# Weight tiles in two transfers of 64 partitions each, in a one-core decoder layer

## The reference, cut to what matters

```
hn = rms_norm(x);   proj = hn @ w_in             # 2048 x 7184
... gated DeltaNet and retention heads on proj ...
h  = x + mixed @ w_out                           # 2048 x 2048
hn = rms_norm(h);   q = hn @ w_pq                # 2048 x 2048, then top 16 of product keys
h  = h + sum_k gelu(expert_u[idx_k] . hn) * gate_k * expert_v[idx_k]     # 16384 experts, 128 picked a token
h  = h + sigmoid(rms_norm(h) @ w_ple_gate) * (p @ w_ple_proj)
out = rms_norm(h)
```

## Time and profile before

| | |
|---|---|
| median of three runs | 2109.89 us (2107.45 to 2109.89) |
| profiled execution, whole | 2103.78 us |
| its span | 2101.9 us |
| TensorE busy | 2039.3 us, 97% |
| VectorE busy | 1638.5 us, 78% |
| ScalarE busy | 1084.8 us, 52% |
| read from HBM | 476.31 MB |
| mean rate of the transfers | 236 GB/s |

### The profile page before, as it was taken

How to read it: one execution, slowest core, us unless ns; L and a number is a source line. 1 busy time by engine, 2 the same in 40 slices (tenths; PEclk the granted TensorE clock), 3 DMA queues, 4 the chain that set the end, 5 groups by cost and what they waited for, 6 DMA issues and landing times.

```text
span 2101.9 us, 38248 instructions
## 1 busy us (share of the span) xinstructions
PE 2039.3 (97%) x12266; PEld 1869.2 (89%) x12266; DVE 1638.5 (78%) x2509; ACT 1084.8 (52%) x1450; POOL 725.3 (35%) x423
## 2 busy tenths in 40 slices
PE   7999999979999999999999999999999999999997
PEld 7888778878789999999999999999999899899785
DVE  6885777985567888888888666898889788888755
ACT  6543566334435755545554544555555555455454
POOL 0030200000001878788888860232323233343000
PEclk9999999999999999999999999999999999999999
DMA  5655558215555777777777776899999889999454
GB/s 196 254 185 184 171 170 298 103 55 206 183 178 176 213 205 208 212 208 209 210 202 209 216 245 244 317 350 348 350 344 346 299 306 330 351 332 341 171 182 138
DMA packets 171795, 496.19 MB, mean 236 GB/s; under 512 B 48560, under 2 KB 48976, under 8 KB 169808
## 3 DMA queue, kind: packets, MB, share of 16 engines
q1 hardware_dynamic: 117056, 413.39, 56.8%
q0 software_dynamic: 51200, 67.25, 12.0%
q10 hardware_dynamic: 3472, 14.78, 1.9%
HBM read 476.31 MB, written 19.04 MB: 236 GB/s over the span
## 4 chain that ended last, share of the span: by engine, by line
PE 81%; DVE 8%; DMA 6%; DVEq 2%; ACT 1%; issue 1%; ACTq 0%; SPq 0%
PE ps L261 27%; PE ps L266 15%; PE ps L1922 14%; PE ps L1927 8%; PE ps L287 5%; PE ps L281 5%; PE ps L282 5%; DMA raw<-in_v_table 4%; DVE lo L241 2%; ACT hi L235 1%; PE ps L363 1%; DMA arena<-in_u_table,few_pick 1%; DVE arena L1133 1%; DMA raw<-in_w_in_cols 1%; DVE arena L1468 1%
## 5 line engine op out<-in xcount | busy, mean ns | idle before, releaser
L235 ACT ACTIVATE hi<-raw 128x1024 fp32r<-128x1024 f32 x724 | 768.5, 1062 | 865.3 <-PE ps L261 387.1
L241 DVE TENSOR_TENSOR lo<-raw,hi 128x1024 fp32r<-128x1024 f32 x724 | 892.3, 1236 | 346.6 <-ACT hi L235 308.8
L261 PE MATMUL ps<-act_pair,hi 128*128 128x448 f32 (+1 forms) x2816 | 654.4, 374 | 0.0
L1653 POOL DMA_INDIRECT gate_map<-gate_in_sb x256 | 473.3, 1849 | 401.3 <-DVEq L1418 325.7
L261 PEld LDWEIGHTS ps<-act_pair,hi 128*128 128x128 f32 x2816 | 504.5, 189 | 49.2
L266 PEld LDWEIGHTS ps<-act_pair,lo 128*128 128x128 f32 x2816 | 372.0, 191 | 18.9 <-DVE lo L241 3.9
L266 PE MATMUL ps<-act_pair,lo 128*128 128x224 f32 (+1 forms) x2816 | 375.3, 276 | 1.9 <-DVE lo L241 1.9
L1922 PE MATMUL ps<-stage,hi 128*128 128x448 f32 x1024 | 232.1, 367 | 3.0 <-ACT hi L235 1.5
L1922 PE MATMUL ps<-act_pair,hi 128*128 128x448 f32 x1024 | 229.7, 366 | 1.9 <-ACT hi L235 1.9
L1670 POOL DMA_INDIRECT arena<-in_u_table,few_pick x64 | 104.4, 1631 | 304.3 <-DVE keep L1468 270.0
L1922 PEld LDWEIGHTS ps<-stage,hi 128*128 128x128 f32 x1024 | 183.1, 189 | 17.6 <-DVE gate_in_sb L1520 2.4
(11 more groups left out here) (254 smaller groups left out, 1678.0 us busy)
## 6 DMA issues: line engine op xcount, KB each, us to landing
raw<-in_expert_u SPq DMA_DIRECT2D x256, 512.0 KB
raw<-in_v_table SPq DMA_DIRECT2D x256, 512.0 KB
raw<-in_w_in_cols SPq DMA_DIRECT2D x64, 512.0 KB
raw<-in_w_in_rows SPq DMA_DIRECT2D x48, 512.0 KB
raw<-in_w_out SPq DMA_DIRECT2D x32, 512.0 KB
raw<-in_w_pq SPq DMA_DIRECT2D x32, 512.0 KB
raw<-in_w_gate SPq DMA_DIRECT2D x32, 512.0 KB
gate_map<-stage SPq DMA_DIRECT2D x1, 14336.0 KB, 41.2
```

The source lines that it names most:

```text
L235: act.activation(hi[:, use, :], raw[:, slot, :], ACT.Copy).then_inc(hi_ready, 1)
L241: dve.tensor_tensor(lo[:, use, :], raw[:, slot, :], hi[:, use, :].bitcast(F32), ALU.subtract).then_inc(lo_ready, 1)
L261: mm = pe.matmul(first_tokens(out_ap), hi[:, use, d8 * P:(d8 + 1) * P], first_tokens(act_pair[:, d, :]), start=(d == 0), stop=False)
L1653: pool.indirect_dma_start(gate_map, bass.IndirectOffsetOnAxis(ap=place[0:n, unit, r:r + 1], axis=0), gates_out[0:n, unit, r:r + 1], None, ...
```

## The change

Each weight tile is fetched by two transfers in place of one: partitions 0 to 63 and then partitions 64 to 127, 256 KB each, both on SyncE's queue and both on the buffer's semaphore. Each raises it by 16, so ScalarE waits for 32 a turn. The tile's place, its bytes, the wait ahead of the transfers and all of the other engines' work stay as they were.

```diff
         def load_tile(sp, n, slot, src, first=False):
             if not first:
                 sp.wait_ge(lo_ready, n - RAW + 1)
-            sp.dma_start(raw[:, slot, :], src).then_inc(weights_landed[slot], 16)
+            for part in range(2):
+                rowsl = slice(part * P // 2, (part + 1) * P // 2)
+                sp.dma_start(raw[rowsl, slot, :], src[rowsl]).then_inc(weights_landed[slot], 16)
 
         def round_tile(act, n, slot, use, turn, first=False):
-            act.wait_ge(weights_landed[slot], 16 * turn + 16)
+            act.wait_ge(weights_landed[slot], 32 * turn + 32)
             if not first:
                 act.wait_ge(hi_used, n - SPLIT + 1)
                 act.wait_ge(lo_ready, n - SPLIT + 1)
```

## The result

The changed kernel took 2324.19 us (median of four runs, 2306.31 to 2334.13) against 2108.67 us of the kernel before: a ratio of 1.101, with a 95% interval of 1.098 to 1.104. It is slower by about 215 us. The forecast of slower held. Its size, 95 us, did not: less than half of the loss was foreseen. That 2324 us lies just inside the likeliest case's 2140 to 2330 is owed to the width of that range and not to the sum.

The account below looks back on a forecast made before the run. TensorE was taken to bound the kernel, with transfers close behind in the second expert stage. Only engine time counted: 54 + 41 = 95 us on 2103.8, plus 4 for the median, gave 2203 us; range 2103 to 2330.

Parts of the forecast that it names:

- the likeliest case: Engine time of the halves shows in part, mainly in the second expert stage: 2140 to 2330 us, chance 0.50.
- What bounds the kernel, and where it shows: Whole kernel: TensorE, busy 97%, sets the pace; in the second expert stage transfers are close behind, DMA 0.95 and 0.91.
- SyncE: SyncE's queue: issues double to 1448, 0.5 us more a tile, covered by 2.2 us of standing still; 0 on the path.
- The later half: Every tile: upper half issued 0.5 us later, hidden by the 1.9 us reserve; taken as 0, at worst 44 us.
- more completions: Every tile: one more small packet per engine, at most 0.16 us a tile; taken as 0.
- The engine time of the bytes: DMA engines, every tile: bytes to few partitions hold an engine longer, 0.07 us per 4096 B, 0.55 us a tile.
- What of it lies on the path: Second expert stage: 0.55 us less idle 0.13 and 0.23 us, times 128 tiles each: 54 and 41 us, sum 95.
- The cover elsewhere: Outside the second expert stage: idle engine time hides the 0.55 us, barely in the first expert stage (0.63 us a tile).
- nothing happening: Whole kernel: rival that the halves run as one transfer did, 2104 to 2111 us, chance 0.24.
- Half rate for all weight bytes: Rival: +1.26 us a tile, 277 us over the second expert stage, 2381 us; chance 0.12 (above 2330).

Follow-up runs that it names:

- e4: Changed kernel, but the second expert stage's 256 tiles come whole and all others stay split into lower and upper halves: 2121.04 us, 1.005 of the kernel before.
- e2: Changed kernel with each tile cut into two column halves of all 128 partitions instead of lower and upper partitions: 2121.41 us, 1.0059 of the kernel before.
- e3: Changed kernel with each tile cut into even and odd partitions instead of lower and upper ones: 2126.64 us, 1.0081 of the kernel before.
- e1: Separate kernel streaming weight tiles without computing, cut in different ways: whole 1.32 us a tile, lower and upper halves 2.23, columns 1.38, even and odd 1.41.
- the mixed streams: Separate transfer-only kernels with 384 KB to 128 partitions beside each tile; on ScalarE's queue, in the later one, all whole 2.25 us, all split 3.45.

## Why the prediction was right or wrong

**What bounds the kernel, and where it shows:** right. TensorE's 97% meant nothing for the second stage, where transfers were close behind; 205 of 213 us arose there, and the first expert stage hid all but 1 us of its cost (e4).

**SyncE:** right. It stood still for 1153.0 us in place of 1549.7, 0.55 us less a tile, for which I had 0.5. One issue of 64 partitions lasted 0.468 us, not the 0.333 I had used.

**The later half and more completions:** I took 0 for both. Together they are at most 11 to 16 us (e2, e3, whose transfers alone are also a little slower than whole ones, 381 and 371 against 397 GB/s), in the lower part of the 0 to 44 that I had bounded. Packets under 512 B rose from 48560 to 60145, by 16 for each of 724 tiles as assumed.

**The engine time of the bytes, the step that failed.** The mechanism was right, the term too small, twice over. First, 0.55 us a tile: transfers alone take 2.23 in place of 1.32 us, 0.91 more (e1). I had measured the price in half a microsecond at which narrow loads began and then mixed with whole tiles, and kept to the milder side. Second, I charged it to the 8 rows of the weight tile in an engine. The row of after gives the price for any 4096 B, 1.03 x 16 x 4.096 / 255 = 0.265 us against 0.180 before (0.95 at 346 GB/s), for 13.3 of them in the first half of the stage (346 GB/s x 2.52 us / 16 / 4096 B), or 1.13 us a tile. The bytes that go to all partitions pay as well, as the mixed streams show: 3.45 - 2.25 = 1.20 us for their 896 KB.

**What of it lies on the path:** this failed too, the other way. I took idle shares of 0.13 and 0.23 us off as the room that there was. At the stream's 407 GB/s the kernel's 0.86 MB would take 2.11 us, so the room was 2.52 - 2.11 = 0.41 us. What the measurements give: 0.86 MB at the 266 GB/s of all split are 3.22 us, and (3.22 - 2.54) x 256 = 174 us; at the 256 GB/s of three in flight 3.35 us and 207 us; 205 were lost. How many of its four buffers the kernel has in flight was not measured. Had I kept my way and put in 0.91, it would have been (0.91 - 0.13) x 128 + (0.91 - 0.23) x 128 = 187 us: near the loss, but only because the wide bytes' price and the greater room, both left out, nearly cancel.

**The cover elsewhere:** the first expert stage as said (0.92, forecast near 0.95). The first 200 us lost 7 us in a stretch that the mean share hid.

**The rivals:** nothing happening is excluded, and so is a count of transfers (e2, e3). Half rate for all weight bytes, 277 us, came nearer to the size than the sum did, though not for its reason; the half rate itself was not reached, since lower and upper halves in turn got 235 and not 209 GB/s. That 40% of the bytes go to all partitions, which I held against it, counted for little.

## What to carry to other kernels

Where a stage's transfers are close to its limit, cut one by columns or by alternate partitions, not into the lower and the upper 64: the number of transfers cost 0.6 to 0.8% here, the choice of partitions 9 to 10%. Before a change that slows transfers, compare the stage's rate with what a bare stream of about the same mixture reaches (346 and 328 against 407 GB/s here), since the DMA share (0.91 to 0.95) doesn't tell how much room is left, nor a stage's mean how full its worst stretch is. And a slow kind of transfer takes the quick ones in the same engines with it: half of the tiles split cost 72% of all split, though a quarter cost 19%.

## What the runs showed of the hardware that I had not expected

- An issue on SyncE's queue lasts longer for half of the partitions: 0.468 us at the median for 64 partitions, 0.475 for even or odd ones, and 0.333 for 128 partitions, whole or in columns. In e1, where issues follow each other closely, the medians are 0.595 and 0.596 for halves of either kind and 0.431 for columns.
- TensorE, kept waiting, was granted a lower clock at times. Over the second expert stage the mean granted clock went from 1.00 to 0.98 (the two rows of the whole stage above), and its busy time rose by 52.5 us for the same instructions. The clock accounts for an estimated 17 us of that (0.02 x 864 us); where the rest comes from stays open. In one window of 4 us in which TensorE was busy 2.40 us the granted clock was 0.84, and in the next 0.73, so it was at its lower level of 1.2 GHz for a part of both:

```profile
1500.00:1504.00 4.00, 2.40 (x10) 2.21 (x10) 2.50 (x3) 1.93 (x3) 0.41 (x1) 0.84 1.02 237
1504.00:1508.00 4.00, 4.00 (x23) 3.86 (x22) 2.79 (x5) 1.71 (x3) 0.39 (x1) 0.73 1.02 275
```

The DMA engines' share was 1.02 in both windows, so the transfers were full there; what the lower clock cost beside them was not tried.
